# Attention on query blocks of 8 rows by 16 columns with 640 keys each, bias tables finished in DRAM, transfers merged

## What is computed

```
def row_block(r):
    r0 = jnp.clip(r - kr // 2, 0, rows - kr)
    k_win = k_band[:, :, :, col_idx]
    ...
    s_win = einsum('bhqd,bhrqcd->bhqrc', q_r, k_win) * scale + bias
    s_ctx = einsum('bhqd,bkhd->bhqk', q_r, k_ctx) * scale
    p = softmax(concatenate([s_win, s_ctx], -1))
    return einsum(p_win, v_win) + einsum(p_ctx, v_ctx)
```

## Time and profile before

| | |
|---|---|
| median of 3 executions | 3200.53 us (3199.91 to 3201.78) |
| the profiled execution | 3199.34 us, of which the span of the trace is 3197.5 us |
| PE busy | 2978.2 us, 93% of the span |
| DVE, ACT, POOL busy | 55%, 25%, 23% |
| convolution | about 125 to 566 us |
| first network | about 660 to 1600 us |
| values, first queries and keys | 1633 to 1800 us |
| attention | 1800 to 2325 us |
| output projection to the end | 2325 to 3197.5 us |

### The profile page before, as it was taken

One profiled execution on the slowest core, in us unless ns is written; L12 is line 12 of the kernel. 1 busy time (PEld: TensorE's weight loads), 2 busy tenths in 40 slices (PEclk: granted clock), 3 DMA queues, 4 the chain that ended last, 5 costly groups with the idle time before them and its releaser, 6 DMA issues.

```text
span 3197.5 us, 44615 instructions
## 1 busy us (share of the span) xinstructions
PE 2978.2 (93%) x15738; PEld 2467.4 (77%) x15738; DVE 1762.4 (55%) x2975; ACT 814.8 (25%) x1425; POOL 737.0 (23%) x457
## 2 busy tenths in 40 slices
PE   5899999689999999999969899999798999999996
PEld 1588888478888888888759788888675888888884
DVE  1645545666666776655551366666614554555556
ACT  1311111321111111111142366666623111111112
POOL 0221111021111111111111254445421222222210
PEclk8899999899999999999989999999998999999998
DMA  9210013021222212211035556555630111111111
GB/s 356 73 53 26 32 46 89 0 69 55 76 72 74 79 55 78 69 44 39 33 95 123 166 144 177 161 160 144 182 138 26 39 52 46 40 59 39 59 39 59
DMA packets 156872, 269.26 MB, mean 84 GB/s; under 512 B 70272, under 2 KB 97920, under 8 KB 156800
## 3 DMA queue, kind: packets, MB, share of 16 engines
q1 hardware_dynamic: 156800, 268.32, 26.8%
HBM read 222.13 MB, written 50.07 MB: 85 GB/s over the span
## 4 chain that ended last, share of the span: by engine, by line
PE 77%; DVE 6%; issue 5%; ACT 4%; DMA 4%; SPq 1%; POOL 1%; DVEq 0%; POOLq 0%; ACTq 0%
PE psum L668 42%; PE psum L699 19%; PE psum L828 4%; PE psum L807 3%; PE psum L882 2%; PE psum L851 2%; PE psum L865 2%; DMA o_dram<-o_st_lo 1%; DVE residual L1343 1%; DVE prod L1323 1%; DMA mod_raw<-mod_panels 1%; PE psum L634 1%; POOL w_lo L1657 1%; ACT squares L982 1%; ACT pt_hi L1158 1%
## 5 line engine op out<-in xcount | busy, mean ns | idle before, releaser
L1343 DVE SCALAR_TENSOR_TENSOR residual<-psum,modulation,residual 128x512 f32<-128x512 f32 (+1 forms) x1072 | 718.2, 690 | 884.5 <-PE psum L699 882.5
L1657 POOL TENSOR_TENSOR w_lo<-raw,w_hi 128x1024 fp32r<-128x1024 f32 x196 | 491.2, 2520 | 1927.9 <-ACT w_hi L976 1925.0
L668 PE MATMUL psum<-act_hi,w_hi 128*128 128x512 f32 (+1 forms) x2208 | 589.2, 367 | 9.5 <-POOL w_lo L1657 7.5
L668 PE MATMUL psum<-act_lo,w_hi 128*128 128x512 f32 (+1 forms) x2208 | 589.3, 367 | 0.0
L668 PE MATMUL psum<-act_hi,w_lo 128*128 128x512 f32 (+1 forms) x2208 | 588.7, 367 | 0.0
L668 PEld LDWEIGHTS psum<-act_hi,w_hi 128*128 128x128 f32 x2208 | 397.7, 188 | 88.3 <-issue 7.7
L976 ACT ACTIVATE w_hi<-raw 128x1024 fp32r<-128x1024 f32 x196 | 204.1, 1061 | 1013.8 <-PE psum L668 938.1
L668 PEld LDWEIGHTS psum<-act_lo,w_hi 128*128 128x128 f32 x2208 | 380.2, 188 | 70.7
L668 PEld LDWEIGHTS psum<-act_hi,w_lo 128*128 128x128 f32 x2208 | 380.3, 188 | 70.5
L699 PE MATMUL psum<-prod_hi,w_hi 128*128 128x512 f32 (+1 forms) x1072 | 408.3, 381 | 28.2 <-DVE residual L1343 10.4
L699 PE MATMUL psum<-prod_hi,w_lo 128*128 128x512 f32 (+1 forms) x1072 | 396.3, 370 | 0.0
(11 more groups left out here) (120 smaller groups left out, 3707.4 us busy)
## 6 DMA issues: line engine op xcount, KB each, us to landing
raw<-ffn_panels SPq DMA_DIRECT2D x132, 512.0 KB, 5.0
mod_raw<-mod_panels SPq DMA_DIRECT2D x48, 512.0 KB, 9.6
mod_in<-mod_rest SPq DMA_DIRECT2D x64, 384.0 KB, 3.1
raw<-conv_panels SPq DMA_DIRECT2D x32, 512.0 KB, 5.2
k_hi<-k_dram SPq DMA_DIRECT2D x32, 320.0 KB, 5.7
k_lo<-k_dram SPq DMA_DIRECT2D x32, 320.0 KB, 7.3
v_st<-v_dram SPq DMA_DIRECT2D x32, 320.0 KB, 7.2
raw<-qk_panels SPq DMA_DIRECT2D x16, 512.0 KB, 4.4
```

Source lines behind the costliest of these rows:

```text
L668: mm = pe.matmul(psum[:, bank + b, 0:tn], w[:, s, kb, :], acts[h][:, kb, t0:t0 + tn], start=(kb == 0 and n == 0), stop=(kb == KB - 1 and n ...
L1343: dve.scalar_tensor_tensor(out=residual[:, ob, t0:t0 + tn], in0=psum[:, 6 + r % 2, 0:tn], scalar=modulation[:, gates + ob, kind_of(t0):kin ...
L1657: pool.tensor_tensor(panel(w_lo, s), raw[:, s], panel(w_hi, s), ALU.subtract).then_inc(lo_done[s], 1)
```

## The change

A half unit is now 8 rows by 16 columns of queries: a unit holds one block of 16 columns, its two halves are the upper and the lower 8 rows of the grid. The columns that 16 neighbouring queries can reach lie in a window of 32, and the rows in a band of 12, so that a half has 12 x 32 = 384 keys and the context, 640 in all. Queries are stored in DRAM by column block; `k_st` is read with the window as a pattern; `v_band` holds a window's values and is loaded by four transfers of 32 partitions each (one for each row of a group of four rows). The groups are three in every unit: four, four and two turned pieces; in the last group each product has 128 columns. The bias table with all masks is built once in DRAM, in 384 columns for each head, half and kind of window: 32 transfers write -1e30 everywhere, and six times in the convolution 16 gathers, a masking addition on POOL and 16 stores put the entries in. High and low parts share a transfer (`q_dram`, `k_dram`, `o_dram`), the output stage is double, and the table of projections is dealt anew. The output projection's addition (L1604 before) goes in pieces of 256 columns instead of 512.

```
+        Q_COLS = WIN_COLS
+        WINDOW, BAND_ROWS = 2 * WIN_COLS, WIN_ROWS + WIN_ROWS // 2
+        BAND_KEYS = BAND_ROWS * WINDOW
+        KEYS = TC + BAND_KEYS
...
-        GROUPS = [OUTER, INNER, INNER, OUTER]
+        SLOTS_OF = [[(0, 1, ((0, BAND + P), (1, BAND))), (2 * P, 2, ((0, BAND + 2 * P), (1, BAND + P)))],
+                    [(4 * P, "c0", ((0, C0), (1, C0))), (6 * P, "c1", ((0, C1), (1, C1)))],
+                    [(8 * P, 0, ((0, BAND),)), (9 * P, 3, ((1, BAND + 2 * P),))]]
+        GROUPS = len(SLOTS_OF)
...
-        QK_CHUNKS = {**chunks(1, 2, 0, (5, 5, 5, 5, 4)), **chunks(1, 3, 6, (6, 6, 6, 6)), **chunks(1, 4, 11, (8, 8, 8)),
-                     **chunks(2, 0, 15, (5, 5, 5, 5, 4)), **chunks(2, 1, 21, (5, 5, 5, 5, 4))}
-        QK_DRAINED = {6: (1, 2), 11: (1, 3), 15: (1, 4), 21: (2, 0), 27: (2, 1)}
+        QK_CHUNKS = {**chunks(1, 2, 0, (8, 8, 8)), **chunks(1, 3, 4, (8, 8, 8)), **chunks(1, 4, 8, (12, 12)),
+                     **chunks(2, 0, 11, (6, 6, 6, 6)), **chunks(2, 1, 16, (5, 5, 5, 5, 4))}
+        QK_DRAINED = {4: (1, 2), 8: (1, 3), 11: (1, 4), 16: (2, 0), 22: (2, 1)}
...
+            sp.wait_ge(pool_step, 9)
+            for h in range(HEADS):
+                for ab in range(2):
+                    sp.dma_start(bias_dram[h, :, ab], blank[:]).then_inc(bias_filled, 16)
+            for j in range(1, KB):
                 for s in range(4):
                     load_panel("conv", s, j, conv_panels[j, s])
+                if j == 2:
+                    sp.wait_ge(bias_filled, 16 * 2 * HEADS)
+                if 0 <= j - 2 < BIAS_STAGES:
+                    store_bias_rows(j - 2)
+                if j - 1 < BIAS_STAGES:
+                    load_bias_rows(j - 1)
...
             def load_bias(i, b):
                 at_least(sp, s_done, 16 * i + 8 * b - 8)
+                sp.dma_start(bias[b][:], bias_dram[2 * i + b]).then_inc(bias_rows_in[b], 16)
...
+            def load_v(i, u):
+                b, j = divmod(u, COL_BLOCKS)
+                at_least(sp, pv_ready, UNITS * i + u + 1 - UNITS)
...
+                for r in range(KEY_ROWS):
+                    src = bass.AP(tensor=v_dram[:].tensor, offset=head + (r * GRID_W + WINDOWS[j]) * row,
+                                  ap=[[row, WINDOW], [KEY_ROWS * GRID_W * row, ROW_TILES], [1, row]])
+                    sp.dma_start(v_band[b][j][r * WINDOW:(r + 1) * WINDOW].bitcast(F32), src).then_inc(v_in[u], 16)
...
             load_heads(0, 0)
-            load_v(0, 0)
+            for u in range(4):
+                load_v(0, u)
             store_qk(1, 0)
...
+                for part in range(2):
+                    rows = k_st[:, b, part, 0:TL].rearrange("p (r c) -> p r c", c=GRID_W)
+                    pe.matmul(psum[:, 2 * ab, 0:BAND_KEYS], q_st[:, b, q0:q0 + P],
+                              rows[:, EDGE * ab:EDGE * ab + BAND_ROWS, WINDOWS[j]:WINDOWS[j] + WINDOW],
+                              start=(part == 0), stop=(part == 1))
...
-                at_least(act, o_out, 32 * (UNITS * i + u))
+                at_least(act, o_out[u % 2], 16 * (UNITS // 2 * i + u // 2))
...
             for s in range(3):
                 split_lo("conv", s, 0)
+            pool.wait_ge(norms[0].summed, SUMS * len(ALL))
+            pool.memset(blank[:], MASKED).then_inc(pool_step, 1)
             norm(0, ALL)
...
-            tables(0, 0)
```

More of the change, by code:

```diff
@@ L140, in trunk @@
+        PT = 2 * P * 5
+        pt_hi, nxt = place("pt_hi", [P, PT], F32R, nxt)
+        pt_lo, nxt = place("pt_lo", [P, PT], F32R, nxt)
+        neg_s, nxt = place("neg_s", [P, 2, KEYS], F32, nxt)
+        bias_0, nxt = place("bias_0", [P, 2, COL_KINDS, BAND_KEYS], F32, nxt)
+        V_PIECE = 4 * ROW_TILES * P
+        v_at = [nxt + V_PIECE * n for n in range(3)]
+        assert v_at[-1] + V_PIECE <= act_at, (v_at, act_at)
         q_st, nxt = place("q_st", [P, 2, TL], F32R, raw_end - SPARE_SLOTS)
@@ new lines, in trunk @@
+        assert v_at[-1] + V_PIECE <= w_hi_end
+        stage, nxt = place("stage", [P, 2, BANK], F32, w_lo_end - SPARE_SLOTS)
+        o_st, nxt = place("o_st", [P, 2, 2, 2 * P], F32, nxt)
+        assert nxt <= w_lo_end, (nxt, w_lo_end)
+        k_st, nxt = place("k_st", [P, 2, 2, T], F32R, scratch_at)
+        v_at.append(nxt)
+        v_band = [[place(f"v_band{b}_{j}", [P, ROW_TILES, P], F32R, v_at[b * COL_BLOCKS + j])[0]
+                   for j in range(COL_BLOCKS)] for b in range(2)]
+        v_ctx_0, nxt = place("v_ctx_0", [P, CTX_TILES, P], F32R, nxt + V_PIECE)
@@ L387, in _, with load_bias_rows @@
                 load_panel("conv", s, 0, conv_panels[0, s])
-            with sp.Fori(1, KB) as j:
+            def load_bias_rows(n):
+                group, kind = divmod(n, COL_KINDS)
+                at_least(sp, bias_out, 16 * ROWS * n)
+                for c in range(Q_COLS):
+                    src = bass.AP(tensor=rpb_padded.tensor,
+                                  offset=group * HEAD_GROUP * REL * PADW + GRID_W - 1 - kind * Q_COLS // 2 - c,
+                                  ap=[[REL * PADW, HEAD_GROUP], [PADW, REL], [1, WINDOW]])
+                    sp.dma_start(bias_stage[c * HEAD_GROUP:(c + 1) * HEAD_GROUP], src).then_inc(bias_in, 16)
@@ new lines, in store_bias_rows @@
+            def store_bias_rows(n):
+                group, kind = divmod(n, COL_KINDS)
+                line = 2 * COL_KINDS * BAND_KEYS
+                sp.wait_ge(bias_masked, n + 1)
+                for row in range(ROWS):
+                    ab, r = divmod(row, WIN_ROWS)
+                    first = min(max(row - EDGE, 0), ROWS - WIN_ROWS)
+                    begin = first - row + WIN_ROWS - 1
+                    offset = (group * HEAD_GROUP * P + r * Q_COLS) * line
+                    offset += (ab * COL_KINDS + kind) * BAND_KEYS + (first - EDGE * ab) * WINDOW
+                    dst = bass.AP(tensor=bias_dram[:].tensor, offset=offset,
+                                  ap=[[line, Q_COLS], [P * line, HEAD_GROUP], [1, WIN_ROWS * WINDOW]])
+                    sp.dma_start(dst, bias_stage[:, begin:begin + WIN_ROWS].rearrange("p r k -> p (r k)")
+                                 ).then_inc(bias_out, 16)
@@ L520, in _ @@
             store_qk(1, 1)
+            for u in range(4, UNITS - 1):
+                load_v(0, u)
             def attention(i, panels=True, heads=True, queries=True):
@@ new lines, in _ @@
+            first, inner, last = (col_mask[:, kind, :] for kind in range(COL_KINDS))
+            keep_where(first[:, 0:half], HEAD_GROUP * half + HEAD_GROUP - 1, HEAD_GROUP, -1)
+            keep_where(inner, HEAD_GROUP - 1, HEAD_GROUP, -1)
+            keep_where(last[:, 0:WIN_COLS], HEAD_GROUP - 1 - HEAD_GROUP * half, HEAD_GROUP, -1)
+            pool.wait_ge(pool_step, 2 + 3)
+            keep_where(first[:, WIN_COLS:WINDOW], -HEAD_GROUP * (WIN_COLS - half + 1), -HEAD_GROUP, 1)
+            keep_where(inner, HEAD_GROUP * (WIN_COLS - 1), -HEAD_GROUP, 1)
@@ L1652, in _ @@
+            keep_where(last[:, WIN_COLS + half:WINDOW], -HEAD_GROUP, -HEAD_GROUP, 1)
+            pool.wait_ge(pool_step, 2 + 6)
             pool.wait_ge(consts, CONSTS)
@@ L1729, in attention @@
                     nxt_i, nxt_u = (i, u + 1) if u < UNITS - 1 else (i + 1, 0)
-                    if u == 0:
-                        tables(i, 1)
-                    if u == 4 and not last:
-                        tables(i + 1, 0)
-                        pool.wait_ge(bias_done, 2 * i + 3)
                     more = not (last and u == UNITS - 1)
```

371 lines of the change are left out of this document (168 added, 203 removed).

## The result

The changed kernel takes 3230.09 us (median of 4 runs, 3228.04 to 3231.89); the kernel before, run beside it, 3201.15. The ratio is 1.0093, with a 95% interval from 1.0081 to 1.0105: 0.9% slower, where 1.5% faster was forecast.

A forecast was written before the change was run, and what follows sets the result against it. PE was taken to bound the six steady pairs, DVE the last. From 3199.3 us, -39.6 - 15 - 4.5 + 7 + 5 + 1 = -46 gave 3153; with the median 1.2 above, 3154, range 3138 to 3188.

The forecast's parts named there:

- Steady pair: Six middle attention pairs: PE work 54.4 us plus 4.7 idle, 59.1 a pair, 6.6 less; -39.6 in all.
- Idle: 3.5 remains: Steady pair: PE's old idle time of 3.5 us a pair stays; the last unit without projections adds 1.2.
- Narrow products: Rival, chance 0.33: value products of 128 columns cost 0.23 us, not 0.0875; +26, so 3180 us.
- Seventh pair: Attention's last but one pair: 55 us instead of 69.8, with 3 left for the store wait; -15.
- last pair: Attention's final pair, without projections: seven steps at 0.7 us less, some lost at the end; -4.5.
- Fill: Blank fill of the DRAM bias tables: 18.9 MB at 406 GB/s delay the convolution's second panels; +7 us.
- Gathers and stores: Bias entries in the convolution: 32 transfers a step at 0.91 us each, done before panels are wanted; hidden.
- Start: Start of attention: first tile's store behind more bias, ACT's last tile behind values; +5 us (2 to 9).
- End: End of the kernel: ACT waits for both halves of the output addition; +1 us.
- No effect: Rival, chance 0.03: DVE or the group chain sets the steady pace, pairs stay near 65; 3195 to 3203 us.
- slower case: Rival, chance 0.04: bias-entry transfers over 1.3 us delay convolution panels, from 1.6 PE loses 10 a step; 3214 us.
- DMA as the bound: Rival, chance 0.12: values at 114 GB/s keep engines busy 57 of 59 us; pairs 62 to 63, 3172 to 3178.

The follow-up runs named there:

- e1: Changed kernel with only the third projection tile's store issued ahead of the values and bias on SP's queue; 3182.63 us, ratio 0.9956.
- e7: Changed kernel with third tile and query tile stored earlier, results loaded in last pair, panels before bias rows, mask behind product, fill in later halves; 3159.78 us.
- e6: Changed kernel with convolution panels issued ahead of the bias transfers and POOL's mask addition held until the product's low part is done; 3227.81 us, ratio 1.0078.
- e10: Kernel before the change with only the loads of the first five pairs' results moved into the last pair; 3202.81 us, ratio 1.0006.
- e11: Kernel before the change with results loaded two pairs at a time behind the last pair's first two stores; 3193.13 us, ratio 0.9981.
- e5: Changed kernel with the second pair's first query tile stored ahead of the first pair's value pieces; 3228.28 us, ratio 1.0077.
- e12: Fastest reordered kernel (3147.93 us) with ACT's copy and DVE's head sum moved ahead of a tile's drain and the second inverse; 3146.23 us, ratio 0.9824.

## Why the prediction was wrong

- **Steady pair.** Forecast 59.1 us, measured 66.8. PE's own sum nearly holds: in e1 it is busy 55.5 us a pair (forecast 54.4) and idle 4.0 (forecast 4.7), and a pair takes 59.5. (The kernel before is busy 63.5 us a pair by the window of its six pairs, where the sum had 62.2, so that 2.2 were idle and not 3.5; this changes little.) The step that failed is "Idle: 3.5 remains". I took what was left of the old idle time and added the unit without projections, but did not follow the store of the third tile past what SP now issues ahead of it. For the queue I had only asked whether its bytes fit into the pair. They do (46 us of 59 forecast, 77.5% of 59.5, also 46, measured in e1), and the pair still lost 7.3 us to the order in which they stand.
- **Narrow products**, the rival with 0.33, didn't come. Four with 128 columns:

```profile
1925.38 0.27 PE L949 MATMUL psum<-pt_lo,v_band 128*128 128x128 f32 x1
1925.49 0.27 PE L949 MATMUL psum<-pt_hi,v_band 128*128 128x128 f32 x1
1925.60 0.27 PE L949 MATMUL psum<-pt_lo,v_band 128*128 128x128 f32 x1
```

  They are 0.11 us apart, between my 0.0875 and the 0.23 of the rival, 0.7 us a pair more. The 384 strided columns took 0.18, as taken.
- **Seventh pair.** Forecast 55, measured 74.1; with the results' loads out of it and the store first (e7), 54.4. Again a queue: "the double stage takes most of the 8.4 away; I leave 3". The second result buffer covers a store that lands within two units, and this one took 22.9 us. The last pair gained 2.2 instead of 4.5.
- **Fill.** Forecast +7, measured 5.6 by the wait alone (6.8, where 1.2 stood before) and 7.6 by what e6 leaves: right, with 396 GB/s for the 406 of the earlier trace rows. By the 358 GB/s that the Trainium skill gives for the HBM traffic of a core (page "SBUF — State Buffer", section A bandwidth-pool intuition that's wrong), it would have been 13, an estimate; the rate in the trace is higher, and decides.
- **Gathers and stores.** "Hidden" was wrong by 5.5 us. The rival on them asked whether the next panels come late for PE, with a threshold of 1.3 us a transfer; they are issued in 0.72 and 0.64 us, well under it. Panels did come later, in time for PE, but POOL then split them beside DVE's taps, and "POOL's six additions lie in a stage where it is idle" forgot that the other engine isn't. In this stage an idle engine's work wasn't free, since both read SBUF.
- **Start** +5, measured 8.8 (6.5 against e10 and e11), inside its bounds of 2 to 9; e5 shows the order of the store to be 5 of it. **End** +1, measured -0.2, within what equal stretches differ by.
- **Rivals.** The result, 3230, lies outside the range, above every case. "No effect" (3195 to 3203) had the size of a held-up pair but laid it to DVE; the slower case (3214) had the right queue and the wrong stage. None let a single store, hidden before, wait behind 1.2 MB. DMA as the bound (0.12) looked at the sum of bytes too.

Shown by runs: the stop, its two parts, the results' loads, both collisions in the convolution, the fill, and that with these moved the change pays. Left open: what made the transfers late that took e12's gain back, and how the gain is shared between the blocks and the rest of the change. A second stage in place of the order, and a fill on another queue, weren't tried.

## What to carry to other kernels

When transfers are merged or reordered on one queue, follow each store whose buffer is single: what is issued ahead of it, how many bytes those are, and how soon the next writer wants the buffer; that the sum of bytes fits says nothing about it. Put stores that free a buffer ahead of loads that are wanted a stage later. And before giving an idle engine new work, look at what its neighbour does in the same microseconds.

## What the hardware showed that I had not expected

- POOL's and DVE's additions from SBUF stretch each other: 1.40 us of mask (1.22 by itself) made three subtractions take 2.65 instead of 1.61, a split of 2.4 us made a tap take 3.46 instead of 1.55; DVE's residual additions, which read PSUM, kept their 0.75 us beside a split.
- fp32r products of 128 columns cost 0.11 us each from start to start, not the price of plain float32.
- A stop of 6 us left PE at 1.2 GHz for 5 us (products of 512 columns 0.42 us apart, 0.23 at the full clock), 2.1 us of busy time a pair; stops of 1.6 us at most, 1.1 a pair, left the clock at 1.00.
